# Prompt attention by pairs of heads in a hybrid decoder step on one core

## What is computed

```python
def block(args):
    qn, qp, i = args
    s = (jnp.einsum('bqhd,bkhd->bhqk', qn, k_nope)
         + jnp.einsum('bqhr,bkr->bhqk', qp, k_pe)).astype(jnp.float32) * MLA_SCALE
    q_pos = i * Q_BLOCK + jnp.arange(Q_BLOCK)
    s = jnp.where(key_pos[None, :] <= q_pos[:, None], s, -jnp.inf)
    p = jax.nn.softmax(s, axis=-1).astype(v.dtype)
    return jnp.einsum('bhqk,bkhd->bqhd', p, v)
```

## Time and profile before

| | us |
|---|---|
| median of three runs | 2453.18 |
| lowest, highest | 2447.33, 2456.1 |
| the profiled execution | 2456.59 |
| its span | 2454.9 |
| PE busy | 2403.7 |
| DVE, ACT, POOL busy | 843.1, 802.9, 835.4 |
| mean granted clock of PE | 0.993 |

### The profile page before, as it was taken

How to read it: one execution, slowest core, us unless ns; L and a number is a source line. 1 busy time by engine, 2 the same in 40 slices (tenths; PEclk the granted TensorE clock), 3 DMA queues, 4 the chain that set the end, 5 groups by cost and what they waited for, 6 DMA issues and landing times.

```text
span 2454.9 us, 40090 instructions
## 1 busy us (share of the span) xinstructions
PE 2403.7 (98%) x15520; PEld 2178.6 (89%) x15520; DVE 843.1 (34%) x1893; ACT 802.9 (33%) x1634; POOL 835.4 (34%) x442
## 2 busy tenths in 40 slices
PE   8999999999999999999999999999999999999998
PEld 8999988986556899998889999888999879999987
DVE  4232200586431432331044232104466644332201
ACT  5223212514332532232253222224322344222222
POOL 3333333230221243333324333332344223333332
PEclk9999999999998999999999999999999999999999
DMA  3222222231541222222222222221211332222322
GB/s 123 81 86 77 94 85 78 69 116 52 164 139 47 70 85 83 85 85 86 83 72 86 79 85 87 85 86 60 90 61 52 132 100 81 84 85 77 94 80 87
DMA packets 65689, 211.91 MB, mean 86 GB/s; under 512 B 8380, under 2 KB 17085, under 8 KB 65310
## 3 DMA queue, kind: packets, MB, share of 16 engines
q1 hardware_dynamic: 62494, 199.70, 26.2%
q0 software_dynamic: 3072, 10.49, 1.5%
HBM read 202.34 MB, written 7.82 MB: 86 GB/s over the span
## 4 chain that ended last, share of the span: by engine, by line
PE 88%; DVE 5%; ACT 3%; issue 1%; DMA 1%; POOL 1%; SPq 0%; DVEq 0%; ACTq 0%; POOLq 0%
PE psum L1717 18%; PE psum L1718 18%; PE psum L1719 18%; PE psum L1849 7%; PE psum L1850 7%; PE psum L1851 7%; PE psum L1842 2%; PE psum L1843 2%; PE psum L2119 1%; PE psum L2056 1%; PE psum L2201 1%; PE psum L2038 1%; ACT y L623 1%; DVE y L1151 1%; PE psum L1992 1%
## 5 line engine op out<-in xcount | busy, mean ns | idle before, releaser
L1008 POOL TENSOR_TENSOR w_lo<-raw,w_hi 128x1024 fp32r<-128x1024 f32 (+1 forms) x317 | 760.2, 2401 | 1372.6 <-ACT w_hi L609 1372.5
L1717 PE MATMUL psum<-x_hi,w_hi 128*128 128x320 f32 (+1 forms) x3312 | 986.2, 298 | 0.2
L1719 PE MATMUL psum<-x_hi,w_lo 128*128 128x320 f32 (+1 forms) x3312 | 981.2, 296 | 0.0
L1718 PE MATMUL psum<-x_lo,w_hi 128*128 128x320 f32 (+1 forms) x3312 | 981.2, 296 | 0.0
L1717 PEld LDWEIGHTS psum<-x_hi,w_hi 128*128 128x128 f32 x3312 | 629.9, 190 | 4.3 <-issue 1.8
L1718 PEld LDWEIGHTS psum<-x_lo,w_hi 128*128 128x128 f32 x3312 | 629.8, 190 | 0.2
L1719 PEld LDWEIGHTS psum<-x_hi,w_lo 128*128 128x128 f32 x3312 | 629.7, 190 | 0.0
L609 ACT ACTIVATE w_hi<-raw 128x1024 fp32r<-128x1024 f32 (+1 forms) x323 | 339.9, 1054 | 833.7 <-DMA raw<-ffn_out 377.1
L1229 DVE TENSOR_TENSOR work<-psum,r_pre 128x256 f32<-128x256 f32 (+1 forms) x352 | 160.5, 458 | 657.7 <-PE psum L1719 655.2
L1849 PE MATMUL psum<-w_hi,gu_hi 128*128 128x512 f32 x704 | 275.0, 391 | 0.6
L1850 PE MATMUL psum<-w_hi,gu_lo 128*128 128x512 f32 x704 | 274.1, 389 | 0.0
(11 more groups left out here) (278 smaller groups left out, 2164.6 us busy)
## 6 DMA issues: line engine op xcount, KB each, us to landing
raw<-ffn_in SPq DMA_DIRECT2D x176, 512.0 KB, 3.6
raw<-ffn_out SPq DMA_DIRECT2D x88, 512.0 KB, 3.6
raw<-gla_in SPq DMA_DIRECT2D x25, 512.0 KB, 3.6
cache<-cache SPq DMA_DIRECT2D x64, 160.0 KB, 2.8
cache<-cache_r POOLq DMA_DIRECT2D x64, 160.0 KB, 2.9
raw<-mla_wo SPq DMA_DIRECT2D x8, 512.0 KB, 3.6
raw<-gla_wo SPq DMA_DIRECT2D x8, 512.0 KB, 3.6
st_s<-state_gla SPq DMA_DIRECT2D x8, 512.0 KB, 5.9
```

Of the source, the lines that this page charges most:

```text
L1008: pool.tensor_tensor(w_lo[slot][:, 0:w], raw[slot][:, 0:w], w_hi[slot][:, 0:w].bitcast(F32), ALU.subtract).then_inc(s_lo, 1)
L1717: pe.matmul(out, wh, xh, start=start, stop=False)
L1718: pe.matmul(out, wh, xl, start=False, stop=False)
L1719: return pe.matmul(out, wl, xh, start=False, stop=stop)
```

## The change

Attention goes by pairs of heads. Window `w` is now head `2 * (w // 8) + w % 2` and block `w % 8 // 2`, so neighbouring windows are the same block of two heads. `scores` is called at even `w` only and issues two windows: the two nope products, then the two rotary products, one on rows 0 to 63 and one on rows 64 to 127. For this `kpe` is written to both row halves and `qpe` holds odd heads in rows 64 to 127, in half of the space; the two memsets go. Two heads' outputs are issued at the first two windows of the next pair, and for the last pair behind the loop. The softmax scale goes into the gain of the query norm, so the exponentials have scale 1.0; the maximum is written negated and line 1415 goes (in the decode part it multiplies by -1.0). The page loads' conditions follow the new order. In the diff, "..." marks what is left out; the decode part's two exponentials have scale 1.0 as well, and `s_max` goes.

```diff
@@ -133,7 +133,7 @@
-        qpe = sb("qpe", [P, HEADS, TOK], offset=g_at + 8 * W4)
+        qpe = sb("qpe", [P, HEADS // 2, TOK], offset=g_at + 8 * W4)
@@ -418,6 +418,10 @@
+        def window(w):
+
+            return 2 * (w // (2 * QB)) + w % 2, w % (2 * QB) // 2
+
@@ -434,7 +438,7 @@
-                return max(x % HEADS if x < 2 * HEADS else HEADS - 1 for x in held)
+                return max(x if x < HEADS else min(2 * (x - HEADS) + 1, HEADS - 1) for x in held)
@@ -443,7 +447,7 @@
-                            eng.wait_ge(s_s, QB * (last_head(b, g) + 1))
+                            eng.wait_ge(s_s, 2 * QB * (last_head(b, g) // 2 + 1))
@@ -818,7 +822,7 @@
-                        n = (w % QB + 1) * P
+                        n = (window(w)[1] + 1) * P
@@ -827,11 +831,11 @@
                         act.activation(prob[:, w % LOOK, 0:n], bank[S_BANK[w % LOOK]][:, 0:n], ACT.Exp,
-                                       bias=soft[:, 1, w:w + 1], scale=MLA_SCALE,
+                                       bias=soft[:, 1, w:w + 1], scale=1.0,
                                        accum_out=soft[:, 2, w:w + 1]).then_inc(s_exp, 1)
...
                         v = w - 2
-                        hd, i = v // QB, v % QB
+                        hd, i = window(v)
                         act.wait_ge(s_t, v + 1)
@@ -841,8 +845,9 @@
-                    if w % QB == QB - 1 and w > QB:
-                        out_hi(w // QB - 1)
+                    if w > 2 * QB and w % (2 * QB) in (2, 3):
+                        out_hi(2 * (w // (2 * QB) - 1) + w % 2)
+                out_hi(HEADS - 2)
@@ -1037,12 +1042,6 @@
-                        pool.memset(kpe[ROPE:P, :], 0.0).then_inc(s_zero, 1)
-                        pool.wait_ge(s_zero, 2)
-                    if j == MLA_IN + HEADS:
-                        pool.wait_ge(s_lo, n0 + j + 1)
-                        pool.memset(qpe[ROPE:P, :, :], 0.0).then_inc(s_zero, 1)
-                        pool.wait_ge(s_zero, 3)
@@ -1290,7 +1289,7 @@
-                dve.tensor_scalar(mla_g[:, 0:QT], mla_g[:, 0:QT], float(Q_LORA) ** 0.5, None, ALU.mult).then_inc(s_mg, 1)
+                dve.tensor_scalar(mla_g[:, 0:QT], mla_g[:, 0:QT], float(Q_LORA) ** 0.5 * MLA_SCALE, None, ALU.mult).then_inc(s_mg, 1)
@@ -1322,8 +1321,9 @@
-                dve.tensor_tensor(kpe[0:ROPE, :], t_k[0], t_k[1], ALU.add).then_inc(s_kpe, 1)
-                dve.wait_ge(s_kpe, 1)
+                for e in range(2):
+                    dve.tensor_tensor(kpe[ROPE * e:ROPE * e + ROPE, :], t_k[0], t_k[1], ALU.add).then_inc(s_kpe, 1)
+                dve.wait_ge(s_kpe, 2)
@@ -1367,7 +1367,8 @@
-                        dve.tensor_tensor(qpe[0:ROPE, hd, H[hf]], ta, tb, ALU.add).then_inc(s_rope, 1)
+                        e = ROPE * (hd % 2)
+                        dve.tensor_tensor(qpe[e:e + ROPE, hd // 2, H[hf]], ta, tb, ALU.add).then_inc(s_rope, 1)
@@ -1375,7 +1376,7 @@
-                                        qpe[0:ROPE, hd, SEQ:TOK].rearrange("p (b t) -> p b t", t=DEC_SEQ)
+                                        qpe[ROPE * (hd % 2):ROPE * (hd % 2) + ROPE, hd // 2, SEQ:TOK].rearrange("p (b t) -> p b t", t=DEC_SEQ)
@@ -1403,26 +1404,24 @@
                     if w < ATT:
-                        i = w % QB
+                        i = window(w)[1]
                         n = (i + 1) * P
...
                         dve.wait_ge(s_msk, w + 1)
-                        dve.tensor_reduce(soft[:, 0, w:w + 1], sc[:, 0:n], AX.X, ALU.max).then_inc(s_max, 1)
-                        dve.wait_ge(s_max, w + 1)
-                        dve.tensor_scalar(soft[:, 1, w:w + 1], soft[:, 0, w:w + 1], -MLA_SCALE, None,
-                                          ALU.mult).then_inc(s_neg, 1)
+                        dve.tensor_reduce(soft[:, 1, w:w + 1], sc[:, 0:n], AX.X, ALU.max, negate=True).then_inc(s_neg, 1)
                     if w >= 1:
-                        n = ((w - 1) % QB + 1) * P
+                        n = (window(w - 1)[1] + 1) * P
                         dve.wait_ge(s_exp, w)
...
                         dve.tensor_scalar(pr, pr, soft[:, 3, w - 1:w], None, ALU.mult).then_inc(s_pn, 1)
-                    if w % QB == 0 and w >= 2 * QB:
-                        out_low(w // QB - 2)
+                    if w > 2 * QB and w % (2 * QB) in (3, 4):
+                        out_low(2 * (w // (2 * QB) - 1) + (w + 1) % 2)
+                out_low(HEADS - 2)
                 out_low(HEADS - 1)
@@ -1458,7 +1457,7 @@
-                    dve.tensor_scalar(soft[:, 1, w:w + 1], soft[:, 0, w:w + 1], -MLA_SCALE, None,
+                    dve.tensor_scalar(soft[:, 1, w:w + 1], soft[:, 0, w:w + 1], -1.0, None,
@@ -1973,19 +1972,23 @@
-                pe.wait_ge(s_zero, 3)
+                pe.wait_ge(s_kpe, 2)
                 def scores(w):
-                    hd, i = w // QB, w % QB
+                    hd, i = window(w)
                     n = (i + 1) * P
-                    out = bank[S_BANK[w % LOOK]][:, 0:n]
-                    if w >= LOOK:
-                        pe.wait_ge(s_exp, w - LOOK + 1)
-                    pe.matmul(out, qn[:, hd, i * P:n], kn[:, hd, 0:n], start=True, stop=False)
-                    pe.matmul(out, qpe[:, hd, i * P:n], kpe[:, 0:n], start=False, stop=True).then_inc(s_s, 1)
+                    for e in range(2):
+                        if w >= LOOK:
+                            pe.wait_ge(s_exp, w + e - LOOK + 1)
+                        pe.matmul(bank[S_BANK[(w + e) % LOOK]][:, 0:n], qn[:, hd + e, i * P:n], kn[:, hd + e, 0:n],
+                                  start=True, stop=False)
+                    for e in range(2):
+                        r = slice(ROPE * e, ROPE * e + ROPE)
+                        pe.matmul(bank[S_BANK[(w + e) % LOOK]][:, 0:n], qpe[r, hd // 2, i * P:n], kpe[r, 0:n],
+                                  start=False, stop=True).then_inc(s_s, 1)
                 def head_out(hd):
-                    pe.wait_ge(s_pt, QB * (hd + 1))
+                    pe.wait_ge(s_pt, 2 * QB * (hd // 2 + 1) - 1 + hd % 2)
                     if hd >= 2:
@@ -1994,24 +1997,23 @@
                 bank_free(S_BANK[0])
+                bank_free(S_BANK[1])
                 scores(0)
-                bank_free(S_BANK[1])
-                scores(1)
                 pe.wait_ge(s_evicted, u0 + M_O)
                 scores(2)
-                scores(3)
                 for w in range(ATT):
-                    if LOOK <= w + 2 < ATT:
+                    if LOOK <= w + 2 < ATT and w % 2 == 0:
                         scores(w + 2)
+                    if w >= 2 * QB and w % (2 * QB) < 2:
+                        head_out(2 * (w // (2 * QB) - 1) + w % 2)
                     pe.wait_ge(s_pn, w + 1)
...
                         pe.wait_ge(s_pt, w - 1)
-                    for kt in range(w % QB + 1):
+                    for kt in range(window(w)[1] + 1):
                         last = pe.transpose(bank[2 + w % 2][:, kt * P:(kt + 1) * P],
...
                     last.then_inc(s_t, 1)
-                    if w % QB == 1 and w > QB:
-                        head_out(w // QB - 1)
+                head_out(HEADS - 2)
                 head_out(HEADS - 1)
```

More of the change, by code:

```diff
@@ L252, in hybrid_step @@
         s_kpe, s_rt, s_rope, s_qpes, s_zero = sem("s_kpe"), sem("s_rt"), sem("s_rope"), sem("s_qpes"), sem("s_zero")
-        s_s, s_msk, s_max, s_neg = sem("s_s"), sem("s_msk"), sem("s_max"), sem("s_neg")
+        s_s, s_msk, s_neg = sem("s_s"), sem("s_msk"), sem("s_neg")
         s_exp, s_rec, s_pn, s_t, s_pt = sem("s_exp"), sem("s_rec"), sem("s_pn"), sem("s_t"), sem("s_pt")
@@ L868, in mla @@
                         act.wait_ge(s_fill, 5 * bp)
-                    act.activation(p_new[:, :], p_new[:, :], ACT.Exp, bias=soft[:, 1, w:w + 1], scale=MLA_SCALE,
+                    act.activation(p_new[:, :], p_new[:, :], ACT.Exp, bias=soft[:, 1, w:w + 1], scale=1.0,
                                    accum_out=sums[:, bp, GROUPS:GROUPS + 1]).then_inc(s_exps, 1)
                     for f in range(GROUPS):
-                        act.activation(p_s[:, f, :], bank[f], ACT.Exp, bias=soft[:, 1, w:w + 1], scale=MLA_SCALE,
+                        act.activation(p_s[:, f, :], bank[f], ACT.Exp, bias=soft[:, 1, w:w + 1], scale=1.0,
                                        accum_out=sums[:, bp, f:f + 1]).then_inc(s_exps, 1)
```

## The result

The changed kernel takes 2462.22 us, the median of 8 runs from 2458.78 to 2466.68; the kernel before took 2453.14 beside it. The ratio is 1.0041, with a 95% interval from 1.0031 to 1.0050: **9.1 us slower**, where the forecast was 2460 us. The profiled execution took 2465.72 us, its span 2464.1. That is 9.2 above the span before, so the two traces can be laid side by side.

What follows compares the result with a forecast made beforehand. PE, busy 98% of the span, bounds the kernel, but in prompt attention PE and DVE wait in a loop. Attention +6.0 and the part before it +0.5 give +6.5 us: 2460 us, range 2455 to 2466, with rivals 2447 to 2469.

Steps and rivals of the forecast that it cites:

- The order of PE's work: Prompt attention: scores issued only at even windows make the PE and DVE loop serial, 17.66 us per pair against 16.44.
- i = 1: Attention loop, block index 1, between ends of successive pairs' transposes: scores, then DVE's normalisation, then transposes in series, 3.90 us.
- i = 2: Attention loop, block index 2, same end-to-end measure: scores, DVE's normalisation and transposes in series, 4.87 us.
- i = 3: Attention loop, block index 3, same measure: the next pair's scores are short, so DVE sets the step, 2.82 us.
- i = 0: Attention loop, block index 0, same measure: scores, two switches, both heads' outputs and transposes, DVE wait covered, 6.07 us.
- the stage: Prompt attention as a whole: decode starts at 638.6 instead of 632.57 us, +6.0 us.
- rival 4: PE's gaps lower its granted clock; chance 0.03, size not given in the text.
- Projections: Before attention: without the memset, POOL's subtractions move and meet other DVE additions, +0.5 us, bounds -1 and +2.
- 1, PE stays covered: Attention: PE is the bound and DVE's reaction is hidden, about -6 us, 2447 us; chance 0.12.
- 2, the halves run serially: Rotary products on the row halves run one after the other, +8.2 us, 2461.5 us; chance 0.13.
- 3, pages late: Cache pages arrive late for decode's transposes; at 2.2 us a page about 5 us more, 2465 us; chance 0.08.
- The negation: Attention: 32 small DVE instructions go, 0.11 us of path each, already counted in the loop's sums.

Runs made afterwards that it cites:

- e4: The kernel before with the softmax scale in the query norm and the maximum negated, nothing else: 2452.98 us, ratio 1.0001 to the kernel before.
- e2: The changed kernel with rotary products on the full array, old qpe layout, one kpe addition and both memsets: 2462.45 us, ratio 1.0043 to the kernel before.
- e3: The changed kernel with the edits of e1 and e2 together, scores earlier and full-array rotary products: 2453.45 us, ratio 1.0005 to the kernel before.
- e1: The changed kernel with each pair's scores issued one window earlier, nothing else: 2451.56 us, ratio 0.9994 to the kernel before.
- e5: The changed kernel with two idle memsets on POOL where the memset of qpe stood: 2461.8 us, ratio 1.0043 to the kernel before.
- e7: The changed kernel with three unread 512-column products added in PE's last two gaps: 2462.77 us, ratio 1.0040 to the kernel before.
- e8: The changed kernel with scores one window earlier, the second kpe half copied by ACT, and idle POOL memsets: 2448.52 us, ratio 0.9989 to the kernel before.
- e9: The same kernel as e8, run again on another chip: 2448.84 us, ratio 0.9988 to the kernel before.

## Why the prediction was right or wrong

**The order of PE's work** was named as the part that decides, and it is. From e4 to e2 the order is added and attention grows from 63.8 to 73.6 us. Issuing the scores earlier takes it back, 8.8 us on the full array (73.6 to 64.8, e3) and 11.8 on the row halves (76.1 to 64.3, e1). By its steps (end of one pair's transposes to the next), forecast against the starts of the scores L1983 in PE's timeline, which lie at the same place of each step:

```
          forecast  measured
i = 1       3.90      4.01   609.38 to 613.39
i = 2       4.87      4.96   595.31 to 600.27
i = 3       2.82      2.88   600.27 to 603.15
i = 0       6.07      6.23   603.15 to 609.38
sum        17.66     18.08
```

The method holds better than its total. The same terms give e2, which was never forecast: no switches (4 x 0.11 less on the path) and one more two-block product (0.43 more) make 17.65, measured 17.61.

**What was mis-sized is the stage, +6.0 us; the trace has +9.8.** Laid along the forecast's own working, the 3.8 us are these. To the end of the first two transposes: +0.1. ACT's table load takes 1.28 us in both traces, from 564.70 before and from 568.28 in the changed kernel, and the first exponential and the first normalisation follow it. The first pair, put at 11.6 us (568.2 to 579.8): 585.07 - 571.83 = 13.2 us, +1.6, and the granted clock was 0.50 in a part of it (573 to 575 us). The next three pairs, put at 52.8: 639.59 - 585.07 = 54.5, +1.7. Of that 3 x 0.42 = 1.3 is in terms that I mis-sized: behind products on row halves the mask starts 0.30 us after their end, not 0.20 (twice a pair on the path); the switch back takes 0.20, not 0.11, and the first head's output product right behind it 2.26 us, where e2 has 2.15. The rest is the clock in the last windows: e5, with the same code and a clock of 1.00 there, is 0.4 us faster in them. From the last transposes to decode: 645.99 - 639.59 = 6.4 against 6.0, +0.4, again the clock, for the outputs take 5.01 us where I had 2.16 + 2.44 = 4.60.

**The clock** was my rival 4, with 0.03. In the kernel before, waits for the normalisation, at the longest 1.2 us for a weight load and 0.8 for a product, leave the granted clock at 1.00 from 564 to 632 us, while behind the gap of 3.41 us it is 0.50 from 543.8 to 546 us. From this I had taken gaps of about 1 us to be harmless. In the steady loop that is so (1.00 behind gaps of 1.07 and 1.16 us). At the first pair and in the last windows it is not always so: the changed kernel fell to 0.57 at the tail and e5 stayed at 1.00 behind the same gaps. Among my signs of being wrong stood "a clock under 1.0 inside the stage", and it came, at the stage's two ends. By an estimate it cost 2.5 us of the 9.8: 1.4 in the first pair, whose step i = 1 took 577.28 - 571.83 = 5.45 us in place of 4.01, and 1.1 at the tail. It is not what makes the loop serial. I should have judged this rival at the stage's two ends as well.

**Projections: +0.5 forecast, about +1.5 and +1.3 found in the trace.** The 1.5 (first kn eviction) is inside my bounds of -1 and +2: a subtraction of POOL moved into the memset's place, as the text said. The 1.3 behind it is the clock once more: the products behind PE's gap at the first kn eviction stayed at a granted clock of about 0.50 longer, to 552 us in the changed kernel, some 5.9 us behind the gap, and to 547 before, some 3.2 us; at 0.50 products of 512 columns start every 0.43 us (546.65, 547.08), at 1.00 every 0.23 (562.85, 563.08). The gap had grown from 3.41 to 3.72 us, but its length does not explain it, for e5 has 3.73 us and only 23.9 behind it. e7, with the same code up to here, shows both again (51.5 and 24.9), but e1, with the same code too, shows 50.5 and 23.8. So neither comes in every execution, and e5, which mends the first, leaves the median where it was.

**Taken together**, the terms found are +9.8, +1.5 and +1.3. Against them stand -3.4 us in stretches that the change does not touch or, as in decode, only in a constant and in when pages are loaded (decode -1.3, the next stretch -1.6, the end -1.3, the start +0.8), of the size by which equal code differs between these traces. That terms of 12.6 us stand beside a span longer by 9.2 is chance in these two executions; the medians differ by 9.1 too, so the two terms of the projections can't be counted in full. The range held, and the likeliest single class, no change within 0.3%, was missed by 0.11%: +9.1 us came where +6.5 was forecast, 2.6 too low.

**The other rivals.** 1, PE stays covered: refuted for this order by the gaps of 1.07 and 1.16 us; largely true once the scores go earlier, in e1, where one gap of 0.98 us is left. It would have given 2447 us; e1 gives 2451.56, since the halves save little there. 2, the halves run serially: refuted by 1.06 us for four instructions. Full overlap of row halves was my estimate from two column halves; the four took 0.20 us more than the 0.86 of full overlap and 0.66 less than the serial 1.72. The 2461.5 us of this rival lie nearer to the measured 2462.22 than my 2460, so the time alone would not have told the two apart. 3, pages late: refuted. One of POOL's page issues of the changed kernel:

```profile
637.41 0.54 POOL L458 DMA_DIRECT2D cache<-cache_r  x1 [1.01 <-issue]
```

They come every 1.55 us, as forecast, though from 635.86 and not from 627.8 on, as everything stands some 8 us later; the last transposes of the first batch pair wait for nothing but DVE's copy:

```profile
662.19 1.06 PE L2040 MATMUL psum<-ident,cache 128*128 128x128 f32 x8 [0.27 <-DVE c_t L1432]
```

Decode got no longer (137.4 us against 138.7).

**The signs.** Mask to mask over a pair was to be about 17.7 us and is 18.08; the gaps before the odd transposes were to be about 1.3 us and are 1.07 and 1.16. "Well over 20 us" of waits for the normalisation did not come: PE's weight loads waited 17.6 us for it where they had waited 14.4, and what grew was the wait of the products themselves, 3.3 to 13.0 us.

**The negation** was forecast at 0.11 us of path a window, 0.17 with the earlier reciprocal. In the trace of e4 the path from the mask to the normalisation takes 596.39 - 595.65 = 0.74 us where it took 595.47 - 594.55 = 0.92, 0.18 less: right in its size. The reciprocal starts 595.99 + 0.29 - 596.20 = 0.08 us before the maximum ends, where I had put 0.06 by an estimate. A head gains 0.31 (8.22 to 7.91), for a transpose behind it takes 0.11 us on the chain where it took 0.23, and eight heads gain 2.5 us, though this isn't seen in the median.

## What to carry to other kernels

Before you make an engine's work smaller, look at who waits for whom around it: where two engines wait for each other, the period is the sum of a path and not the load of the busier one, and work taken off that engine is worth nothing (here some 8.6 us of it, an estimate). When operations are grouped, ask what was running while the other engine worked and whether it still is; here grouping the scores by pairs cost about 10 us, and issuing the same group one window earlier gave it back. And when you price such a loop, price its first and its last turn apart from the steady ones. Last, before you read a difference of a few us out of medians, look at the granted clock by stretches: one stretch of code that no kernel here changed took 6.5 us more or less.

## What the runs showed of the hardware

- Products on 64 rows, in turn on the two row halves, run at once: four instructions of 512 columns in 1.06 us to the next shape, against 1.71 for four on the full array. With the overlap taken as full (0.86 us, an estimate), the switch back to the full array takes 0.20 us, and the consumer (VectorE's mask) starts 0.30 us after their end, 0.10 later than behind a full-array product. Both matter only where a consumer waits.
- PE's granted clock fell behind gaps of at most 1.2 us (0.57 in 637 to 641 us, behind gaps of 1.16 and 0.98 us with only transposes between) and stayed at 1.00 through a loop with gaps of 1.07 and 1.16 us with scores and outputs between (590 to 630 us).
- The same code behind the same gaps can run at either level: the tail at 0.57 in one execution and at 1.00 in another (the changed kernel and e5), and the start of the output projection at 0.55 and 1.00 in two executions of one kernel (e8 and e9), which is 6.5 us.
- A VectorE addition of two SBUF operands (64x320) that starts behind a running GpSimd subtraction ended 0.35 us after it in the three cases above (0.48 us became 2.6 to 2.7); beside a GpSimd memset one took its own 0.49 us, and a VectorE product with one operand in PSUM took its own 0.49 us beside a subtraction.
- A maximum that comes out negated costs what a plain one costs (0.29 us for one block, 0.69 for four).
